# A mixture-of-experts stage on one core: the last block on four units, fewer table forms, and three weight pieces requested early

## What is computed

```python
def _moe(h, router_g, router_e, w1, w3, w2):
    g_val, g_idx = lax.top_k(jax.nn.softmax(hf @ router_g), 1)            # one of 4 groups
    e_logits = take_along_axis(hf @ router_e, g_idx)                      # its 8 experts
    e_val, e_idx = lax.top_k(jax.nn.softmax(e_logits), TOP_K)             # two of them
    gate = g_val * e_val / jnp.sum(e_val, axis=-1, keepdims=True)
    ...
    def block(args):
        tok, e = args
        xb = h[tok]
        return (jax.nn.silu(xb @ w1[e]) * (xb @ w3[e])) @ w2[e]
```

## Time and profile before

| | us |
|---|---|
| median of 3 launches | 1469.42 (1469.12 to 1469.8) |
| time of the profiled launch | 1473.97 |
| its span | 1472.1 |
| PE busy | 1368.9 (93%) |
| VectorE busy | 671.2 (46%) |
| POOL busy | 566.1 (38%) |
| ScalarE busy | 309.4 (21%) |
| moved by the transfers | 318.04 MB, mean 216 GB/s |

### The profile page before, as it was taken

The page is one execution under the profiler, slowest core; times in us unless marked ns, Lnnn a source line. Parts: engine busy times, 40 slices in busy tenths (PEclk is TensorE's granted clock), DMA queues, the critical chain, the costliest instruction groups (busy, mean ns, idle before and its releaser), DMA issues. The chain is left out here.

```text
span 1472.1 us, 33644 instructions
## 1 busy us (share of the span) xinstructions
PE 1368.9 (93%) x13661; PEld 960.7 (65%) x13661; DVE 671.2 (46%) x1362; ACT 309.4 (21%) x843; POOL 566.1 (38%) x452
## 2 busy tenths in 40 slices
PE   8999999998998999999999858999999989999864
PEld 4678888865566668887777534666666766666641
DVE  4757787842325567666667471112112111111127
ACT  1311011113113444443443100011001001100015
POOL 4212423402223235543334012445545544445435
PEclk9999999999998999999999979999999999999987
DMA  6334333244136232213321199999999999999936
GB/s 250 89 97 99 76 78 102 61 121 160 47 110 245 90 100 80 86 66 115 115 94 44 72 396 376 388 399 399 396 396 404 395 395 398 395 395 395 392 87 237
DMA packets 129606, 318.04 MB, mean 216 GB/s; under 512 B 48120, under 2 KB 86512, under 8 KB 103672
## 3 DMA queue, kind: packets, MB, share of 16 engines
q1 hardware_dynamic: 109720, 294.35, 53.3%
q0 software_dynamic: 18656, 18.15, 5.7%
q10 hardware_dynamic: 1152, 4.52, 0.8%
HBM read 277.05 MB, written 47.74 MB: 221 GB/s over the span
## 5 line engine op out<-in xcount | busy, mean ns | idle before, releaser
L2660 PE MATMUL bank<-sb_arena 128*32 128x256 f32 x6144 | 341.5, 381 | 12.2 <-DVE sb_arena L2768 5.7
L2660 PEld LDWEIGHTS bank<-sb_arena 128*32 128x32 f32 x6144 | 222.9, 111 | 125.4 <-issue 13.2
L515 PE MATMUL bank<-sb_arena 128*128 128x276 f32 x1008 | 235.0, 395 | 0.0
L2631 POOL DMA_INDIRECT d_acc<-sb_arena,sb_oidx x96 | 152.1, 1584 | 194.0 <-ACT sb_arena L2726 166.0
L515 PEld LDWEIGHTS bank<-sb_arena 128*128 128x128 f32 x1008 | 191.0, 190 | 44.0
L2676 PE MATMUL bank<-sb_arena 128*32 128x256 f32 x3072 | 172.9, 379 | 7.7 <-ACT sb_arena L2726 7.6
L2676 PEld LDWEIGHTS bank<-sb_arena 128*32 128x32 f32 x3072 | 110.6, 110 | 66.4 <-ACT sb_arena L2726 9.9
L2624 POOL DMA_INDIRECT sb_arena<-d_x,sb_idx x99 | 102.6, 1037 | 109.4 <-DVE sb_idx L2754 51.8
L2773 DVE TENSOR_SCALAR sb_oidx<-sb_slot 128x3 int32 x32 | 5.6, 174 | 286.1 <-DMA d_acc<-sb_arena,sb_oidx 285.7
L2726 ACT ACTIVATE sb_arena<-bank,sb_arena 128x256 f32<-128x256 f32 x96 | 38.5, 472 | 397.1 <-DVE sb_arena L2774 387.7
L1281 PE MATMUL bank<-sb_arena 128*128 128x512 f32 (+1 forms) x256 | 119.7, 596 | 0.0
(11 more groups left out here) (420 smaller groups left out, 1842.5 us busy)
## 6 DMA issues: line engine op xcount, KB each, us to landing
sb_arena<-w SPq DMA_DIRECT2D x192, 1024.0 KB, 28.1
sb_arena<-w_conv SPq DMA_DIRECT2D x28, 512.0 KB, 4.8
sb_arena<-d_conv SPq DMA_DIRECT2D x7, 1792.0 KB, 7.3
d_conv<-sb_arena SPq DMA_DIRECT2D x22, 512.0 KB, 3.3
sb_arena<-d_gam SPq DMA_DIRECT2D x8, 768.0 KB, 5.2
d_x<-sb_arena SPq DMA_DIRECT2D x9, 512.0 KB, 2.6
sb_arena<-xT ACTq DMA_DIRECT2D x8, 552.0 KB, 9.3
sb_arena<-w_out SPq DMA_DIRECT2D x8, 512.0 KB, 7.9
```

Of the source, the lines that this page charges most:

```text
L515: last = e.matmul(bank[at + t][:, 0:HT // 2], weights[:, k, :], x[:, k, HT // 2 * t:HT // 2 * t + HT // 2], start=(k == 0), stop=(k == HK ...
L2631: e.indirect_dma_start(rows_out, bass.IndirectOffsetOnAxis(ap=oidx[:, r:r + 1], axis=0), eo[:, r, :], None, bounds_check=LAST_ROW, oob_is_ ...
L2660: mm = e.matmul(bank[UPB + r][j * CG:(j + 1) * CG, 0:2 * P], xgT[:, 2 * q + k, r * CG:(r + 1) * CG], w13[s][q][:, k, j, :], start=(q == 0 ...
```

## The change

Three things are changed.

1. **The last block has four units.** One expert with 97 to 128 rows is taken as the wide one: all its rows are in one last block of four units on one load of weights (`END_SET`). There is no part block. The wide block's fourth unit has a gather of its own (`xg_end`), issued early; its results, 128 rows, stay in `eo_last`, in the layout 128 rows by 1024, and aren't scattered. Every other expert has one block in the order of its number, and blocks behind it for more rows.
2. **Fewer forms for the tables.** Since an expert's first block stands at its number, the place of a row is found from the group and expert index (`first_at`), and only rows beyond 96 are shifted (`shift`). The lists on one partition are shorter; `free13` and `free2` are made earlier.
3. **Three of the first expert's weight pieces** are requested by SP in step 2 of the chunk loop. To make room, `ch` and `spread` move to the start of that stage's arena, which is where the first weight set will lie.

```diff
@@ chunk loop
+        early = [A(P, KT * 2 * P) for _ in range(EARLY)]
+        A = Arena()
+        ch = [A(P, SB, P) for _ in range(4)]
+        spread = [A(TS, SB, P) for _ in range(2)]
...
                 for i in range(1, NTT + 2):
+                    if i == 2:
+                        for c in range(4):
+                            e.wait_ge(S[f"ch_st{c}"], 32)
+                        e.wait_ge(S["ss_ps"], 8)
+                        for q in range(EARLY):
+                            e.dma_start(early[q], a["w13"][0, q]).then_inc(W["w13" + "abcd"[q] + "0"], 16)
@@ routing stage
-                    for q in range(4):
+                    for q in range(EARLY if s == 0 else 0, 4):
...
+                e.tensor_scalar(spans, iota[:, 0:E], -float(BLK), float(BLK * (E - 1)), ALU.mult, ALU.add)
+                step(e.tensor_scalar(col[1], col[7], -float(BLK * EPG), float(BLK * (EPG * EPG + EPG)), ALU.mult, ALU.add))
+                for j in range(2):
+                    e.scalar_tensor_tensor(first_at[:, j, :], col[8 + j], -float(BLK), col[1], ALU.mult, ALU.add)
...
-                step(e.tensor_scalar(star, number, part_of[:, 0:1], float(PAD), ALU.is_equal, ALU.mult))
-                step(e.tensor_tensor(count, upto_t[:, :, NTT - 1], star, ALU.add))
+                step(e.scalar_tensor_tensor(over, count, float(WIDE), over, ALU.is_le, ALU.mult))
+                step(e.tensor_reduce(wide_of, over, AX, ALU.max))
+                step(e.tensor_scalar(star, number, wide_of[:, 0:1], None, ALU.is_equal))
...
-                e.tensor_tensor(before_t, before_t, bc1(base, P, NTT, E), ALU.add).then_inc(S["r_before"], 1)
+                step(e.scalar_tensor_tensor(el, before_t, float(BLK), bc1(shift, P, NTT, E), ALU.is_ge, ALU.mult))
+                e.tensor_tensor(before_t, before_t, el, ALU.add).then_inc(S["r_before"], 1)
...
+                step(e.tensor_tensor(dest, dest, first_at, ALU.add))
@@ expert stage, PE
-                with e.Fori(E1, last) as b:
+                for n in range((E2 - 2) // NSET * NSET + 1, E2):
+                    up(n, n % NSET, n // NSET + 1)
+                    down(n - 1, (n - 1) % NSET, (n - 1) // NSET + 1)
+                with e.Fori(E2, last) as b:
                     up(b, UP_SET, b)
                     down(e.snap(b - 1), DOWN_SET, b)
+                down(e.snap(last - 1), UP_SET, E2 // NSET + 1)
                 e.wait_ge(S["e_xT"], last + 1)
                 e.wait_ge(S["e_hm"], last)
                 for q in range(4):
+                    e.wait_ge(W["w13" + "abcd"[q] + str(END_SET)], 16 * (E1 // NSET + 1))
                     for k in range(2):
...
+                        for r in range(NR + 1):
+                            for j in range(4):
+                                mm = e.matmul(bank[UPB + r][j * CG:(j + 1) * CG, 0:2 * P], xgT[:, 2 * q + k, r * CG:(r + 1) * CG], w13[END_SET][q][:, k, j, :],
...
-                down(e.snap(last - 1), UP_SET, E1 // NSET + 1)
                 e.wait_ge(S["e_hT"], last + 1)
...
+                        for d in range(2):
+                            mm = e.matmul(bank[UPB + d][:, :], hT[:, c, :], w2[END_SET][h][:, k, d * 512:(d + 1) * 512], start=(c == 0), stop=(c == 3))
@@ expert stage, VectorE
                 x_flip(last)
                 gate(before)
                 mark(two_before)
                 h_flip(before)
-                gate(last)
                 mark(before)
-                h_flip(last)
+                gate(last, units=NR + 1)
+                h_flip(last, units=NR + 1)
```

More of the change, by code:

```diff
@@ new lines, in _ @@
+                e.tensor_scalar(table[0:1, 0:1], total, float(E1), None, ALU.add)
+                for k in range(2):
+                    e.tensor_scalar(ends[0:1, k:k + 1], total, float(E1 - 1 - k), None, ALU.add)
+                e.tensor_scalar(order[0:1, NBMAX:NBMAX + 4], iota[0:1, 0:4], 0.0, float(NBMAX), ALU.mult, ALU.add)
+                done[0] += 1
+                step(e.scalar_tensor_tensor(oseq, turn, total, iota[0:1, E:E + NX], ALU.is_lt, ALU.mult))
+                e.scalar_tensor_tensor(order[0:1, E1:NBMAX], is_end, end_of[0:1, 0:1], oseq, ALU.mult, ALU.add)
@@ L2713, in _, with tanh @@
                 last = last_block(e)
-                def tanh(n, first=False):
+                def tanh(n, first=False, units=NR):
                     e.wait_ge(S["e_up"], 4 * n + 4)
@@ L2728, in _ @@
                 tanh(0, first=True)
-                with e.Fori(1, last + 1) as b:
+                with e.Fori(1, last) as b:
                     tanh(b)
                     evict(e.snap(b - 1))
+                evict(e.value_load(ends[0:1, 0:1], min_val=E1 - 1, max_val=REST - 2))
+                tanh(last, units=NR + 1)
                 e.wait_ge(S["e_og"], last + 1)
-                e.wait_ge(S["e_zero"], 1)
                 e.wait_ge(S["e_out"], 2 * last + 2)
-                for j in range(2):
-                    part = slice(j * CG, (j + 1) * CG)
-                    e.activation(eo_last[part, j * 256:(j + 1) * 256], bank[LAST][part, 0:256], ACT.Copy, scale=gsel_last[part])
+                e.activation(eo_last[:, 0:512], bank[UPB][:, :], ACT.Copy, scale=tok_last[:, 1:2])
             @block.vector
```

236 lines of the change are left out of this document (110 added, 126 removed).

## The result

| | us |
|---|---|
| median of 20 launches after | 1473.34 (1468.90 to 1477.33) |
| median of 20 launches before, same chip | 1469.37 (1462.88 to 1472.37) |
| ratio | 1.0027 (95% interval 1.0018 to 1.0037) |
| profiled launch after | 1469.81, span 1467.9 |
| forecast | 1467.6 (1462.8 to 1471.6) |

A forecast was written before the change was run, and what follows sets the result against it. The ring of eviction, scatters, landing and mark was taken to bound the expert stage; 1472.1 - 2.0 + 1.75 - 1.6 = 1470.25 us of span, 1.85 less, taken from the median 1469.42: 1467.6 us, range 1462.8 to 1471.6.

The forecast's parts named there:

- Routing table: Routing stage: more work ahead of the block list, shorter table-making behind it; ends 2.0 us sooner (bounds 0.8 and 2.6).
- Early pieces: Three weight requests moved to SP's second step, 7.9 us of transfer: gain 0, upper bound 7.9.
- The ring's turns: Expert stage: evict, three scatters, landing, mark, evict again; 16.3 us a turn, expected to stay so.
- a stop at the end: Rival: TensorE's 3.40 us stop falls behind down 30, plus 1.4 slow start: +4.8, 1472.4 us; chance 0.11.
- The last blocks: Serial end from the wait ahead of down 30 to the combining stage, which begins at 1435.1 instead of 1433.35: +1.75 us.
- a sooner landing: Ahead of down 30: the last block's gather no longer runs beside block 28's scatter; 1.2 of 2.2 us taken as gain.
- start of down 30: After the mark at 1400.61 and the eviction from 1401.07 for 1.20 us: 1402.3, before the sooner landing is taken off.
- handing over: Between up 31 and down 31: tanh, two gate operations and flip on four units, plus 0.3: 3.3 us.
- the rest: Behind down 31: eviction in two halves 0.7 us and change of stage 1.4 us.
- the 2.0 for the idle time of 11 us: Cold start of down 30 after TensorE's idle wait: 2.0 us, chosen between 1.4 and 3.1.
- Combining stage: TensorE arrives warm, so its first products run faster; half of 3.1 us passed on: -1.6 (between 0 and 3.1).

The follow-up runs named there:

- rolled: Changed kernel with blocks 28 to 30 as a tenth loop turn instead of written-out blocks, without the loop for further blocks; 1469.25 us, ratio 1.0004.
- unrolled: Kernel before with the last turn of TensorE's expert loop (three blocks) written out behind the loop; 1472.57 us, ratio 1.0025.
- warm_short: Changed kernel with 12 and 3 unused products in TensorE's waits ahead of down 30 and down 31; 1469.55 us, ratio 1.0008.
- up_first_rolled: Changed kernel with the last up phase ahead of down 30 and blocks 28 to 30 as a tenth loop turn; 1463.20 us, ratio 0.9972.

## Why the prediction was wrong

By its parts, with the traces' pieces (means of the like kernels where there are several):

- **Routing table, -2.0:** right, -2.6 (A to B 36.6 and 34.0 in every trace), its upper bound.
- **Early pieces, 0:** right within what can be told. The three requests go out from 479.48 us, right behind the load of the channels at 478.98, and have landed after 12.0 us, where 7.9 were counted; that is still ahead of 499.3, where the products that need the tile begin.
- **The ring's turns, unchanged:** this is the step that failed. The prediction looked for a stop of TensorE only on the serial end. It said of the stop behind the loop: "Now the branch stands ahead of up 30, and 11 idle us swallow it." It gave 0.11 to a stop at the end, and 0 to code anywhere else. The loop ends ahead of up 28, not up 30, since 28 and 29 are written out (the diff says so). They stand in a ring that has no such idle time, and each landing of a scatter during their code is longer by 1.4 us, with packets of an instruction queue in it; a term for this is missing from the sum. Measured: **+3.6 us**, alone in the kernel before and taken back in the changed one. The Trainium skill (Runtime: NRT & Kernel Launch, section on instruction fetch mechanics) says that a taken branch breaks the fetching ahead. The traces agree in part: eleven of the fifteen have a stop of 2.5 to 3.7 us behind the end of the loop, `rolled` and the three traces with written-out blocks in front have none that shows, and none tells which code was fetched. The prediction had the place of the stop wrong; but the time went into the longer landings, and by the turns of `unrolled` the stop adds 0.3 us at most.
- **The last blocks, +1.75:** the order and the places were right (idle 11.7 us ahead of down 30; gate, flip and down 31 with nothing beside them), the sum too small. Ahead of the mark, 1.2 us were to be gained by a sooner landing: block 28's last scatter was issued 12.2 us before the mark (1388.4 in the earlier trace rows, 1400.61), and is 11.7 us before it, 0.5 gained. Behind the mark +2.95 was summed, and is +3.8 in the first pair: start of down 30 1.7, measured 1.9; down 30 7.4 and 6.7 (7.6 to 7.7 in the three further traces); up 31 14.1 and 14.0; handing over 3.3 and 3.0; down 31 7.1 and **8.75** (8.83 in the further ones); the rest 2.1 and 2.2. So +3.3 in all in the first pair; over all like traces, three and four, mark to combining stage and E to F are both longer by 5.0 (32.3 and 37.3; 30.5 and 35.5). The mis-sized term is the clock: the 2.0 for the idle time of 11 us was about right (1.5 to 2.5), but nothing was counted for the 3 us that the same text sets ahead of down 31, though its own row of 3.40 us idle had cost 1.4. That is +1.6 to 1.7. Without the two waits' cold starts the end is 3.2 us shorter by the ratios and 4.1 by the medians (`warm_short`). The Trainium skill (TensorE: Matmul & The Clock Gate, section on HAM oscillation) says that a wait between bursts of products lets the clock fall; it was cited for the first wait only, and the trace agrees for both, with 0.50 behind the one and 0.52 behind the other.
- **Combining stage, -1.6:** -1.9 in the first pair, but 38.0 and 37.5 (F to G) as means over four traces without and five with the change, -0.6. The figure rested on one execution's cold first product.

From A to the end the means of three traces before (the first three of the table) and two after are 624.1 and 629.8, +5.7 us, 1.7 more than the medians. The time ahead of A goes up and down by 9 us from launch to launch, which isn't explained, and five traces are few, so this difference stays open.

So the change loses 3.6 us by written-out code and 3.3 to 5 us at the end, 3.2 to 4.1 of them by the clock; it gains 2.6 in the routing stage and some 0.6 in the combining stage. The same four-unit block with its up phase ahead of down 30 makes 1459 to 1460 us.

## What to carry to other kernels

When a transfer's landing sets the pace, look at what else comes over the queues in those turns: here blocks written out ahead of or behind a loop came with packets of an instruction queue, and nothing in the program's text shows it. Ask of every wait of TensorE what could run in it that is ready; a phase put behind a wait pays for the wait, for its own length, and for the clock. And compare traces from the last common point before the change, not from zero.

## What the runs showed of the hardware

- A landing of scatters in which one or two packets of an instruction queue fall (0.03 MB for two) took 12.0 us from issue to mark instead of 10.6, 30 cases against 258 without, and the two sets don't overlap (11.6 at least, 11.5 at most).
- TensorE stopped for 2.5 to 3.7 us some 36 product records behind the end of a long loop, with `issue` as the reason, in eleven of fifteen traces: at 1333.0 here, at 1338.7 in `unrolled` (38 records), in up 31 at 1386.6 in `up_first_rolled`, and, before, where the earlier trace rows show it. The three traces with written-out blocks in front have no such stop, and in `rolled`, where an idle time of 9.7 us stands near that place, no stop shows.
- The clock was at half behind an idle time of 3.0 us, after 14.0 us of products at full clock (0.52 over the 3.5 us behind it, 8.75 to 8.83 us for the phase in four traces); with 3 idle products in that time the phase took 7.13 us, not 8.75.
- One more indirect transfer early in GpSimd's queue moved an 8 us stop from the 114th to the 91st transfer and made a second at the 169th.
